# A fill tile, the memory norms and the memory heads' score rows change places in a two-block transformer kernel

## The reference, cut to what matters

```python
q = (rmsnorm(q_lat, q_norm_g) @ w_uq).reshape(B, S, N_HEADS_MLA, QK_HEAD_DIM)
kv = (rmsnorm(kv_lat, kv_norm_g) @ w_ukv).reshape(B, S, N_HEADS_MLA, QK_NOPE_DIM + V_HEAD_DIM)
...
q = rope_tail(rmsnorm(q, q_head_g), cos, sin)
k = rope_tail(rmsnorm(k, k_head_g), cos, sin)
o_attn = blocked_bidirectional_attention(q, k, v) * jax.nn.silu(g_attn)
o_conv = c_b * centred_short_conv(c_c * c_u, conv_w, conv_b) * jax.nn.silu(g_conv)
mkv = (rmsnorm(mem, mem_norm_g) @ w_mkv).reshape(B, M, N_HEADS_MEM, 2 * MEM_HEAD_DIM)
m_k, m_v = split_cols(mkv, (MEM_HEAD_DIM, MEM_HEAD_DIM))
mq = rmsnorm(q_mem.reshape(B, S, N_HEADS_MEM, MEM_HEAD_DIM), mem_q_g)
m_k = rmsnorm(m_k, mem_k_g)
s = jnp.einsum('bshd,bmhd->bhsm', mq, m_k).astype(jnp.float32) * (MEM_HEAD_DIM ** -0.5)
p = jax.nn.softmax(s, axis=-1).astype(m_v.dtype)
o_mem = jnp.einsum('bhsm,bmhd->bshd', p, m_v).reshape(B, S, MEM_WIDTH) * jax.nn.silu(g_mem)
```

## Time and profile before

| | |
|---|---|
| median of 3 runs | 2350.02 us (2343.98 to 2350.64) |
| the profiled execution | 2343.68 us, of which the span of the trace is 2341.9 us |
| granted TensorE clock, mean | 0.99 |
| PE busy | 2267.2 us, 97% of the span |
| first block | about the first 500 us |
| gates scattered by POOL | about 1052 to 1800 us |
| value products of the experts | from 1827 us to the end, 502 us |

### The profile page before, as it was taken

The page is one execution under the profiler, slowest core; times in us unless marked ns, Lnnn a source line. Parts: engine busy times, 40 slices in busy tenths (PEclk is TensorE's granted clock), DMA queues, the critical chain, the costliest instruction groups (busy, mean ns, idle before and its releaser), DMA issues.

```text
span 2341.9 us, 29754 instructions
## 1 busy us (share of the span) xinstructions
PE 2267.2 (97%) x9712; PEld 1764.8 (75%) x9712; DVE 1276.6 (55%) x2373; ACT 901.0 (38%) x1419; POOL 1265.7 (54%) x807
## 2 busy tenths in 40 slices
PE   7999999999989999899999999999999999999998
PEld 5666666677767776678888888888887888888887
DVE  4265433214731357388676666322222888888887
ACT  3545543335643444333333332322223333333333
POOL 2342022234434221328888888888887656656563
PEclk9999999999999999999999999999999999999999
DMA  6555123334522111223676666666666999999996
GB/s 216 190 169 192 59 83 99 104 90 128 178 73 90 46 46 37 90 73 64 135 148 141 147 144 148 144 144 144 111 111 140 329 322 353 354 352 356 352 356 244
DMA packets 229714, 392.31 MB, mean 168 GB/s; under 512 B 77665, under 2 KB 153441, under 8 KB 229377
## 3 DMA queue, kind: packets, MB, share of 16 engines
q1 hardware_dynamic: 151296, 323.89, 42.5%
q0 software_dynamic: 78336, 67.45, 14.8%
HBM read 330.21 MB, written 61.01 MB: 167 GB/s over the span
## 4 chain that ended last, share of the span: by engine, by line
POOL 27%; PE 24%; issue 5%; DVE 2%; DMA 1%; ACT 0%; DVEq 0%; POOLq 0%; SPq 0%
POOL gates L976 27%; PE bank L1325 21%; PE bank L1097 2%; DMA tail<-hidden_of_last_block,low 0%; DVE low L1773 0%; ACT staged L1367 0%; DVE h_low L1795 0%; DMA hidden_of_last_block<-staged 0%; DMA gates<-low 0%; POOL tail L1024 0%; DMA tail<-gates 0%; DVE tail L2011 0%; DVE tail L2009 0%; DVE tail L2012 0%; DVE u_split L2044 0%
## 5 line engine op out<-in xcount | busy, mean ns | idle before, releaser
L976 POOL DMA_INDIRECT gates<-low x384 | 633.3, 1649 | 139.0 <-issue 116.7
L1314 PE MATMUL bank<-h_high,u_tiles_split 128*128 128x512 f32 x2048 | 630.8, 389 | 1.2 <-ACT low L1652 1.2
L948 POOL TENSOR_TENSOR u_split<-blocks,u_split 128x1024 fp32r<-128x1024 f32 (+1 forms) x105 | 257.1, 2448 | 675.4 <-ACT u_split L1460 644.3
L1097 PE MATMUL bank<-h_high,u_split 128*128 128x512 f32 (+1 forms) x1712 | 566.2, 405 | 23.2 <-DVE h_low L1795 17.8
L1325 PE MATMUL bank<-v_split,a_split 128*128 128x512 f32 x2286 | 518.7, 389 | 4.4 <-DVE a_split L2083 4.4
L1325 PEld LDWEIGHTS bank<-v_split,a_split 128*128 128x128 f32 x2286 | 428.9, 188 | 94.1 <-DVE v_split L2080 5.1
L1314 PEld LDWEIGHTS bank<-h_high,u_tiles_split 128*128 128x128 f32 x2048 | 384.4, 188 | 81.2 <-ACT low L1652 1.4
L1097 PEld LDWEIGHTS bank<-h_high,u_split 128*128 128x128 f32 (+1 forms) x1712 | 324.1, 189 | 111.9 <-issue 24.7
L1314 PE MATMUL bank<-h_low,u_tiles_split 128*128 128x512 f32 x1024 | 398.3, 389 | 0.0
L1943 DVE TENSOR_TENSOR u_tiles_split<-tail,u_tiles_split 128x1024 fp32r<-128x1024 f32 x128 | 157.2, 1229 | 363.2 <-ACT u_tiles_split L1632 362.4
L1097 PE MATMUL bank<-h_low,u_split 128*128 128x512 f32 (+1 forms) x728 | 288.3, 396 | 0.0
(11 more groups left out here) (196 smaller groups left out, 2326.9 us busy)
## 6 DMA issues: line engine op xcount, KB each, us to landing
tail<-in_uT SPq DMA_DIRECT2D x128, 512.0 KB, 3.8
tail<-in_v SPq DMA_DIRECT2D x128, 512.0 KB, 5.8
gates<-blocks SPq DMA_DIRECT2D x32, 768.0 KB, 5.8
tail<-gates SPq DMA_DIRECT2D x128, 192.0 KB, 5.9
kept_hidden<-tail SPq DMA_DIRECT2D x96, 192.0 KB, 1.9
tail<-kept_hidden SPq DMA_DIRECT2D x96, 192.0 KB, 6.0
blocks<-in_r SPq DMA_DIRECT2D x24, 512.0 KB, 4.0
blocks<-in_conv SPq DMA_DIRECT2D x16, 512.0 KB, 4.3
```

The source lines that it names most:

```text
L948: nc.gpsimd.tensor_tensor(flat(u, 1)[:, 0:n], ring[:, loads[0] % NW, 0:n], flat(u, 0)[:, 0:n].bitcast(F32), ALU.subtract).then_inc(s_wlo, 1)
L976: nc.gpsimd.indirect_dma_start(gate_elements, bass.IndirectOffsetOnAxis(ap=expert_no[tb][:, k:k + 1], axis=0), expert_gate[tb][:, k:k + 1] ...
L1097: last = mm(ps[0:m, :], flat(u, part)[:, k * m:(k + 1) * m], x, start=(k == 0 and j == 0), stop=(k == nk - 1 and j == 2))
L1314: last = mm(bank[slot % 2][:, :], U4[:, slot, w, k, :], x[:, k, :], start=(k == 0 and x is hh and w == 0), stop=(k == KD - 1 and w == 1))
```

## The change

Three edits in `build_schedule`:

```diff
@@ normed(kind, h)
         if key:
             STEPS.append(("sq", key))
+            STEPS.append(("part", len(PROJ), 0, 2))
+            STEPS.append(("norm", key))
         tile(kind, h, KD, P)
-        if key:
-            STEPS.append(("norm", key))
@@ preparation of head 0
     for i, f in enumerate(prep_mla(0)):
         f()
-        if i not in (1, 2):
+        if i not in (0, 1):
             filler()
@@ for h in range(MEM_HEADS)
         for kb in range(MB):
             columns(a, kb)
+        if h + 1 < MEM_HEADS:
+            rows(a + 1)
         for kb in range(MB):
             STEPS.append(("PV", a, kb))
-        if h + 1 < MEM_HEADS:
-            rows(a + 1)
         STEPS.append(("O", a))
```

## The result

The changed kernel takes 2353.76 us in the median of 17 runs (2349.32 to 2357.03), the kernel before 2345.68 us (2341.25 to 2350.64, 17 runs); the ratio is 1.0029, with a 95% interval of 1.0021 to 1.0038. The forecast had a ratio of 1.0030. On the median of the three runs that were shown with the kernel before, it had put 2357.0 us. Over 17 runs that median is 4.3 us lower, and the changed kernel's time lies 3.2 us under the forecast. By the ratio the change makes the kernel about 6.8 us slower (4.9 to 8.9 us by its interval), and by the difference of the two medians 8.1 us. The interval leaves out 1, so it is slower, by about the 0.3% that the forecast took for the least that can be told.

A forecast was written before the change was run, and what follows sets the result against it. PE, busy 97% of the span, was taken to bound the kernel. Terms −4.2 − 2.8 + 2.7 + 13.8 − 0.7 − 1.8 = +7.0 us on the 2350.02 us median gave 2357.0 us, range 2348 to 2363.

The forecast's parts named there:

- What bounds the kernel: Whole program: PE is busy 97% of the span, so its first-block gain or loss moves everything behind it equally.
- one of the signs that the forecast gave for being wrong: POOL's scatter: its start moving by another amount than the first block's end would show the forecast wrong.
- The filler: Head 0's norm: squares go ahead of ACT's evacuation, so the wait and low clock go, −4.2 us.
- the low clock: Head 0, behind the wait: 1.65 us taken as going too; if it stays, only −2.5 us is left.
- The query norms: Head 2: norms six matmuls into the `qm` tiles; the score-row wait goes, −2.8 us, a new wait comes, +2.7 us.
- what is late next: `qm2` in head 2: `mq1`'s square stands behind ACT's fourth exponential, so PE waits, +2.7 us, bounds nothing to 2.7.
- a second late square: `mq2`'s square in `qm3`: claimed done 1.4 us behind the tile, covered by six matmuls, so no wait.
- The doubled tiles: Head 3: `run` ignores a part's bounds, so four `mk` tiles are computed twice, 3.46 us each, +13.8 us.
- The squares of the memory keys: `mk` tiles: the 0.56 us wait at head 4's score rows goes, −0.7 us; no new wait at `mk1`'s norm.
- The score rows: Memory heads: score rows ahead of value products save 0.6 us in each of three heads, −1.8 us.
- The rival: Head 2: the clock falls behind the new wait, or head 0's low stretch stays; +8.7 us, 2358.7 us, chance 0.2.

The follow-up runs named there:

- the doubling alone: Kernel before, with only the four `mk` tiles computed twice, norms behind the second copy as before: ratio 1.0065 (1.0052 to 1.0078).
- the score rows alone: Kernel before, with only the memory heads' score rows moved ahead of the value products: ratio 0.9987 (0.9977 to 0.9997).
- the third norm later too: Changed kernel with bounded `run` and norms placed where squares are ready, then five slices instead of two ahead of `qm3`'s norm: ratio 0.9945.

## Why the forecast was right, step by step

**What bounds the kernel.** That a gain or loss of PE in the first block reaches the end is shown by the doubling alone: +13.8 us in one head, and a ratio of 1.0065 (12 to 18 us by its interval) over the whole. Read to the letter, one of the signs that the forecast gave for being wrong came all the same: the scatter's start moved by 3.2 us and the first block's end by 5.3. The forecast named that sign without allowing for the clock, whose low stretches between 500 and 1050 us lie at other places in the two executions; the traces give no reason to think that the first block's loss was caught up.

**The filler.** The wait went, no other took its place, and norm to norm is 6.33 us. The term of −4.2 us is right for the execution from which it was worked out. The step that took the low clock as the wait's sure companion was too certain: of the four traces that have this wait, the clock fell in three and not in the one of the score rows alone. By that count the low clock is worth 1.65 us three times in four, and the term is nearer to −3.8 us on the mean; so few traces don't settle it.

**The query norms.** The forecast named what goes (2.8 us) and what is late next (2.7 us). Measured against the kernel with no wait in that head (41.95 us), the old wait had cost 2.7 us (44.65) and the new order costs 3.1 (45.03), with 2.58 us of it idle; the term is +0.4 and not −0.1. Most of the difference is a second late square, of which the forecast said that six matmuls cover it. It is `mq2`'s, in `qm3`:

```profile
245.93 0.63 ACT L1367 ACTIVATE blocks<-blocks 128x512 f32<-128x512 f32 x1
...
246.24 0.39 PE L1097 MATMUL bank<-h_high,u_split 128*128 128x512 f32 x1
246.70 1.10 PE L1164 MATMUL bank<-blocks,low 128*128 128x512 f32 x2
```

The square ends at 246.56, and the norm starts 0.46 us behind the last of the six matmuls, where it is 0.23 in the kernel with no wait (the third norm later too). The record shows no wait, because the modelled end of a matmul covers most of it. PE's next matmul starts 0.53 us behind the norm instead of 0.45.

The cause that was given for the long wait, the square behind four exponentials, held up in part by DVE's normalising beside POOL, is shown by moving POOL's part: 1.16 us of the wait is that. The Trainium skill, SBUF — State Buffer, section SBUF: two separate sides, says that whichever of a VectorE instruction in a two-port mode and a GpSimd instruction starts first has their shared port pair for the whole instruction. No run shows the mode of the normalising, but for the rest the traces agree: in the changed kernel the normalising ended at 235.15 + 1.65 = 236.8 and POOL's instruction at 234.16 + 2.35 = 236.5, and with POOL's part moved it was 238.59 + 2.61 = 241.2 and 238.56 + 2.35 = 240.9.

**The doubled tiles.** +13.8 us, as forecast. The sign of the result lies here: with the `mk` tiles as before the ratio is 0.9967, and with the second copies alone taken away 0.9992, which can't be told from 1.

**The squares of the memory keys.** The forecast said that the wait at head 4's score rows goes and that head 2's new wait has no twin, since a full first copy stands ahead. Both came so (+13.0 for the head, 13.1 forecast). But one sentence was wrong: `mq3` was not squared before `mk0` began. In the changed kernel `mk0` starts at 262.46, and `mq3`'s square is the second of two instructions of ACT at 264.42, behind the Exp of k's norm:

```profile
264.42 1.15 ACT L1367 ACTIVATE blocks<-blocks 96x512 f32<-96x512 f32 x2
```

The first copy hid that too; with a bounded `run` it shows as 2.21 us.

**The score rows.** −2.7 us instead of −1.8. The mechanism was right to the tenth: the second score row starts 1.72 us behind the last transposition rows, the value products 3.2 us (472.09 − 468.88), for which the forecast had 464.5 + 0.5 − 461.77 = 3.2. What was mis-sized is the end with which it was compared: the forecast put the end of the old order at 467.4, by the start of the next tile's record. By an estimate, the last two records there start 0.32 us apart and the second has 0.22 us to run, as between the starts of such records elsewhere: 467.03 + 0.32 + 0.22 = 467.6, while the new order, on the same count, ends at 466.7. The difference is 0.9 us a head, not 0.6, and the measured 17.27 − 16.38 is 0.9.

**The clock.** The rival said that a low stretch may come behind the new wait. In the profiled execution of the changed kernel it did not, nor in the three other traces that have this wait of 2.6 us.

**What was luck.** The sum of +7.0 us came out because two terms were off in opposite directions: the query norms by +0.5 us and the score rows by −0.9. The time of 2357.0 us started from a median of three runs that was 4.3 us too high; the difference of the medians, 8.1 us, is 1.1 more than the sum. The mechanisms of the doubled tiles, which make up the result, and of the two waits that go were right.

## What to carry to other kernels

Before a step is split in two, look whether each kind of work that can go through it knows of the split: a loop that ignores its bounds computes everything twice, without a wait to betray it, and the order of instructions shows it at once. Moving work ahead of a wait pays only as far as its own input is ready; ask, for each moved step, when the engine that feeds it has done what stands ahead of it. And when a useless piece of work is taken out, look at what it had been hiding: here 4.9 of 13.8 us came back as waits until the norms were placed one by one.

## What was unexpected of the hardware

PE's clock does not answer to a wait of a given length in a fixed way. In the traces of this case, with the clock at its upper level before the wait, a wait of 2.37 us at head 0 was followed by a low stretch of 3.4 us in three of four. In head 2 it was two of four behind the old wait of 2.69 us, and none of four behind the new one of 2.58 to 2.60 us. It came behind the wait of 2.21 us in head 3, in the one trace that had it, and not behind those of 1.73 and 1.42 us, one of each. Each time it cost about 1.65 us (7.98 against 6.33 us at head 0, 46.31 against 44.65 us in head 2). That these stretches, and longer ones near 690, 920 and 990 us, make up the spread of some 8 us among runs of one kernel is likely: the four runs of the changed kernel under 2351 us have a mean granted clock of 0.990 or 0.991, the five slowest 0.987 to 0.989, and 0.003 of the time is 7 us. It wasn't tried by an experiment.
